# Two transformer blocks on one core: the mixing norm's scale applied where its products are read, the SSD far product half a piece later, gated rows turned by halves

## What is computed

```
hn = rmsnorm(h, norm_mix_w)                    # h * rsqrt(mean(h^2) + 1e-5) * w
q, k, v, z, xbc, dt_raw = split(hn @ w_in)     # 512, 512, 512, 1024, 1536, 16 columns
att = chunk_band_attention(q, k, v, rel_bias)
xbc = silu(causal_depthwise_conv(xbc, conv_w, conv_b))       # x, B, C
dt  = softplus(dt_raw + dt_bias);  a_cum = cumsum(dt * -exp(a_log))
y   = ssd_scan(x, dt, A, B, C) + d_skip * x    # products in chunks with decay
y   = y * silu(z)
y   = y by 2 groups of 512 * rsqrt(mean(y^2) + 1e-5) * norm_w     # the gated rows
h   = h + concat(att, y) @ w_out
h   = h + relu(rmsnorm(h, norm_mlp_w) @ w_ff1)^2 @ w_ff2
out = rmsnorm(h, norm_final_w)
```

## Time and profile before

| | |
|---|---|
| median of 3 runs | 780.57 us |
| runs | 780.35 to 781.04 us |
| the profiled execution | 780.67 us, span 778.9 us |
| granted PE clock | 0.998 of full |
| busy: PE, DVE, ACT, POOL | 762.0, 513.8, 416.0, 98.3 us |
| mixing norm to the turn of the gated rows | 434 to 548 us of the span |

### The profile page before, as it was taken

One profiled execution on the slowest core, in us unless ns is written; L12 is line 12 of the kernel. 1 busy time (PEld: TensorE's weight loads), 2 busy tenths in 40 slices (PEclk: granted clock), 3 DMA queues, 4 the chain that ended last, 5 costly groups with the idle time before them and its releaser, 6 DMA issues.

```text
span 778.9 us, 12960 instructions
## 1 busy us (share of the span) xinstructions
PE 762.0 (98%) x5014; PEld 670.3 (86%) x5014; DVE 513.8 (66%) x816; ACT 416.0 (53%) x623; POOL 98.3 (13%) x74
## 2 busy tenths in 40 slices
PE   8999999999999999999999899999999999999997
PEld 7998877799978887999787699889777999999996
DVE  6985556666664558477866875787856755555554
ACT  5544445453664553446675567576655544444443
POOL 3341000000100004111300207700000000000002
PEclk9999999999999999999999999999999999999999
DMA  9965643344664544676833554765317575656541
GB/s 334 332 203 177 215 163 108 122 157 121 210 224 160 172 157 160 195 227 197 247 114 104 166 176 151 219 205 173 109 55 219 192 237 191 207 177 211 169 156 55
DMA packets 77659, 139.54 MB, mean 179 GB/s; under 512 B 7184, under 2 KB 15648, under 8 KB 77600
## 3 DMA queue, kind: packets, MB, share of 16 engines
q1 hardware_dynamic: 75744, 132.15, 52.4%
q0 software_dynamic: 1856, 6.57, 2.6%
HBM read 134.90 MB, written 1.06 MB: 175 GB/s over the span
## 4 chain that ended last, share of the span: by engine, by line
PE 87%; DVE 6%; issue 3%; POOL 2%; ACT 1%; DMA 1%; SPq 0%; POOLq 0%; ACTq 0%; DVEq 0%
PE acc L1081 13%; PE acc L1083 13%; PE acc L1082 13%; PE acc L1089 12%; PE acc L1091 12%; PE acc L1090 12%; DVE w_lo L810 2%; PE acc L1369 1%; PE acc L1403 1%; DMA raw<-in_w_in_even 1%; PE acc L1342 1%; PE acc L1282 1%; PE acc L1238 1%; PE acc L1353 1%; POOL b_lo L810 1%
## 5 line engine op out<-in xcount | busy, mean ns | idle before, releaser
L810 DVE TENSOR_TENSOR w_lo<-raw,w_hi 128x1024 fp32r<-128x1024 f32 (+1 forms) x224 | 275.3, 1245 | 171.3 <-ACT w_hi L790 90.2
L1089 PE MATMUL acc<-x_hi,w_hi 128*128 128x256 f32 x840 | 234.8, 280 | 1.5 <-DVE w_lo L810 1.1
L1091 PE MATMUL acc<-x_hi,w_lo 128*128 128x256 f32 x840 | 232.1, 276 | 0.0
L1090 PE MATMUL acc<-x_lo,w_hi 128*128 128x256 f32 x840 | 232.1, 276 | 0.0
L790 ACT ACTIVATE w_hi<-raw 128x1024 fp32r<-128x1024 f32 (+1 forms) x128 | 133.6, 1045 | 126.4 <-PE acc L1091 63.9
L780 ACT ACTIVATE w_hi<-raw 128x1024 fp32r<-128x1024 f32 x109 | 116.1, 1065 | 107.6 <-PE acc L1091 55.5
L1089 PEld LDWEIGHTS acc<-x_hi,w_hi 128*128 128x128 f32 x840 | 157.7, 188 | 4.1 <-issue 2.8
L1090 PEld LDWEIGHTS acc<-x_lo,w_hi 128*128 128x128 f32 x840 | 157.8, 188 | 0.8 <-issue 0.5
L1091 PEld LDWEIGHTS acc<-x_hi,w_lo 128*128 128x128 f32 x840 | 157.7, 188 | 0.0
L1081 PE MATMUL acc<-w_hi,cat_hi 128*128 128x512 f32 x272 | 108.9, 400 | 0.2 <-DVE w_lo L810 0.2
L1083 PE MATMUL acc<-w_hi,cat_lo 128*128 128x512 f32 x272 | 106.2, 390 | 0.0
(11 more groups left out here) (297 smaller groups left out, 903.0 us busy)
## 6 DMA issues: line engine op xcount, KB each, us to landing
raw<-in_w_ff SPq DMA_DIRECT2D x32, 1024.0 KB, 5.3
raw<-in_w_in_even SPq DMA_DIRECT2D x28, 1024.0 KB, 5.0
raw<-in_w_in_odd SPq DMA_DIRECT2D x16, 1024.0 KB, 5.4
raw<-in_w_in SPq DMA_DIRECT2D x16, 1024.0 KB, 5.6
raw<-in_w_out_even SPq DMA_DIRECT2D x12, 1024.0 KB, 5.4
raw<-in_w_out SPq DMA_DIRECT2D x4, 1024.0 KB, 5.3
raw<-in_w_in_even SPq DMA_DIRECT2D x4, 512.0 KB, 6.2
raw<-in_w_ukv_even SPq DMA_DIRECT2D x8, 256.0 KB, 3.2
```

The lines of the kernel that those rows point to most:

```text
L810: ins = eng.tensor_tensor(lo, r, hi.bitcast(F32), ALU.subtract)
L1089: pe.matmul(o, wh[k][:, fs], hi[:, ka, :], start=start and f % 2 == 0, stop=False, skip_group_check=True)
L1090: pe.matmul(o, wh[k][:, fs], lo[:, ka, :], start=False, stop=False, skip_group_check=True)
L1091: ins = pe.matmul(o, wl[k][:, fs], hi[:, ka, :], start=False, stop=stop, skip_group_check=True)
```

## The change

Six things change, all in the second block (and one place of the order, `waiting`, that only concerns it).

1. `mix_turn` turns the unscaled rows of `res`, four tiles to a bank. `row_scaled` is gone. ACT's squares and DVE's mean squares stand behind the splits, POOL takes both roots of the layer norm before both of the mixing norm. The filler is 4 products, ahead of tile 1.
2. r is applied where the products are read. For token-major results (V, z, dt) it is a number for each partition (`mix_r`, for tanh `half_r`). For feature-major ones (convolution, q, k) it is a row, which a product of ones and two diagonals spreads over the partitions (`mix_spread`, one instruction of 256 columns, between the halves of the first convolution chunk; ACT copies it to `r_row`). The convolution's, q's and k's results are now read by DVE.
3. V's products of tile 0's low parts stand between the high ones of tile 1 (`v_rows`); dt is one pass of 256 tokens. The pieces with 256 columns share their place in memory differently (`p.shift`).
4. `ssd_far` is a step of its own behind the second half of the piece around `ssd_rows` 0; on DVE its reading stands behind `masked(0)` and z's product.
5. The gate is two steps: `ssd_gate` (variances and root) and `ssd_scale` (the scalings, in the order 0, 2, 1, 3, behind the piece's second half). `ssd_turn` starts with the first two.
6. The low parts of the two output pieces `w_out`, k0 = 4, are POOL's (`state_out`); DVE's low part of the piece at `ssd_scale` stands behind the scalings, and ACT's high part at `ssd_turn` behind the turned rows' own.

```diff
-BUSY_MIX = (5, 1)
+BUSY_MIX = 4
...
     step("mix_turn", 1)
-    step("rows_of", (rows_pieces["dt"], 0, 0, 8))
     step("rows_of", (rows_pieces["v"], 1, 0, 8))
...
+            step("mix_spread", 0)
             step("dt_sum", c_dt)
...
         two()
+        if ("ssd_rows", 0) in sts:
+            step("ssd_far", 0)
+        if ("ssd_gate", 0) in sts:
+            step("ssd_scale", 0)
...
-            p.shift = (80, 112) if p.chunk.layout == "feat" else (0, 0)
+            p.shift = (80, 112) if p.chunk.layout == "feat" or p.cols == S else (0, 0)
...
+        state_out = [p for p in pieces if p.chunk.acts == "cat2" and p.k0 == 4]
...
-            return 4 if p.chunk.epilogue == "silu_tok" and p.chunk.info["dst"][0] == "zb" else 1 if p.n < 2 else 0
+            return 4 if p.chunk.epilogue == "silu_tok" and p.chunk.info["dst"][0] == "zb" or p in state_out else 1 if p.n < 2 else 0
...
-        waiting = {at for at, (s0, s1) in enumerate(zip(steps, steps[1:])) if s0[0] in ("piece", "rest") and s1[0] in ("scores", "ssd_cb")}
+        waiting = {at for at, (s0, s1) in enumerate(zip(steps, steps[1:])) if s0[0] in ("piece", "rest") and s1[0] in ("scores", "ssd_cb", "ssd_turn")}
...
+                if t == 0:
+                    for b in range(4):
+                        high(0, b)
+                    return
+                for b in range(4):
+                    low(0, b)
+                    high(1, b)
+                for b in range(4):
+                    ins = low(1, b)
...
             def mix_turn(t):
 
                 if t:
-                    pe.wait_ge(*due("mix_lo", 4))
-                    keep_busy(acc[:, v_piece.chunk.pair, 1, :], BUSY_MIX[1])
-                rows = tmp[:, t * D:(t + 1) * D]
+                    keep_busy(acc[:, v_piece.chunk.pair, 1, :], BUSY_MIX)
                 for h in range(2):
-                    pe.wait_ge(*due("mix_scaled", 2 * t + h + 1))
+                    pe.wait_ge(*due("mix_row", 2 * t + h + 1))
...
+                elif kind == "mix_spread":
+                    pe.wait_ge(*due("mix_diag", 1))
+                    own(pe.matmul(aux[:, 3, 0:S], ones, gated[:, 1, :], start=True, stop=True), "mix_spread")
...
                 elif kind == "ssd_turn":
-                    pe.wait_ge(*due("y_gated", 1))
-                    turn_tokens(R2[:, 2048:4096].rearrange("p (t n) -> p t n", t=T), "normed_turned")
+                    for h in range(2):
+                        pe.wait_ge(*due("y_gated", h + 1))
+                        turn_tokens(R2[:, 2048:4096].rearrange("p (t n) -> p t n", t=T), "normed_turned", range(4 * h, 4 * h + 4))
...
             def row_hi(t):
 
                 for b in range(4):
-                    act.wait_ge(*due("mix_turned", 4 * t + b + 1))
+                    act.wait_ge(*due("mix_turned", 2 * t + b // 2 + 1))
...
+                elif kind == "mix_spread":
+                    act.wait_ge(*due("mix_spread", 1))
+                    own(act.activation(r_row, aux[:, 3, 0:S], ACT.Copy), "row_scale")
...
+                    elif c.scaled and c.epilogue == "silu_tok":
+                        act.wait_ge(*due("piece_used", c.pieces[-1].n + 1))
+                        act.wait_ge(*due("mix_half", 1))
+                        for t in range(T):
+                            ins = act.activation(epi_dst(c)[:, t], a2[:, t], ACT.Tanh, scale=half_r[:, t:t + 1])
+                        own(ins, "tanh_ready")
...
                 elif kind == "ssd_turn":
                     turned_hi(TURNS["ssd", 0], ssdn_col, cat2_hi[:, 4:12, :], "normed_hi")
+                    hi_first(act, own, held_hi)
...
-                own(dve.tensor_tensor(y, y, zb[:, i * 512:(i + 1) * 512], ALU.mult))
+                own(dve.scalar_tensor_tensor(y, y, mix_r[:, b:b + 1], zb[:, i * 512:(i + 1) * 512], ALU.mult, ALU.mult))
...
+                            ins = dve.tensor_tensor(conv_in[:, f:f + 2, 3:], a2[:, b, :].rearrange("p (f s) -> p f s", f=2), rows_scale(2), ALU.mult)
...
                     row_add(0, 1)
-                    row_mean_square(0)
                     row_part(0, 1)
                     dve.wait_ge(*due("piece_used", last_out[1].n + 1))
                     row_add(1, 1)
                     row_part(1, 1)
                     row_moments(1)
                     row_centred(1)
-                    row_lo(0, 0, 2)
                     row_normed(1)
-                    row_lo(0, 2, 4)
+                    row_lo(0)
+                    row_mean_square(0)
                     row_mean_square(1)
+                    row_lo(1)
                     low_prep(dt_piece.n)
-                    row_lo(1, 0, 4)
                     low_prep(conv_piece.n)
+                    dve.wait_ge(*due("mix_r", T))
+                    for t in range(T):
+                        ins = dve.tensor_scalar(gated[:, 1, t * P:(t + 1) * P], ident, mix_r[:, t:t + 1], None, ALU.mult)
+                    own(ins, "mix_diag")
+                    own(dve.tensor_scalar(half_r, mix_r, 0.5, None, ALU.mult), "mix_half")
...
                     masked(i)
+                elif kind == "ssd_far":
+                    dve.wait_ge(*due("y_far_ready", 1))
+                    own(dve.tensor_tensor(y_far, aux[:, 2:4, :].rearrange("p c (h n) -> p (c h) n", n=SSD_P),
+                                          ssd_c[:, 7, 16:32].rearrange("p (h n) -> p h n", n=1).to_broadcast([P, 16, SSD_P]), ALU.mult),
+                        "far_read")
+                    own.wait()
+                    own(dve.tensor_tensor(y_ssd[:, 1], y_ssd[:, 1], y_far, ALU.add))
...
+                elif kind == "ssd_scale":
+                    y2 = R2[:, 2048:4096]
                     dve.wait_ge(*due("y_rstd", 1))
-                    for n in range(4):
+                    for n in (0, 2, 1, 3):
                         v = y2[:, n * 512:(n + 1) * 512]
-                        own(dve.tensor_scalar(v, v, ssd_c[:, 3, 12 + n:13 + n], None, ALU.mult), "y_gated" if n == 3 else None)
+                        own(dve.tensor_scalar(v, v, ssd_c[:, 3, 12 + n:13 + n], None, ALU.mult), "y_gated" if n > 1 else None)
+                    low_of(*held_low)
+                    held_low = None
...
                         inverse_root(stats[:, 44 + t:45 + t], stats[:, 36 + t:37 + t], "mix_rstd")
+                    for t in range(T):
                         pool.wait_ge(*due("mix_mean", t + 1))
```

More of the change, by code:

```diff
@@ L141, in __init__ @@
         self.banks = None
+        self.scaled = False
 def plan(w):
@@ L547, in build @@
     by_turn = {c.turn: c for c in chunks if c.turn is not None}
-    READER = {"keep_ranks": "act", "copy_tok": "act", "copy_feat": "act", "conv_in": "act", "copy_dt": "dve"}
+    after_mix = min(c.n for c in chunks if c.epilogue == "copy_dt") - 1
+    for c in chunks:
+        c.scaled = c.acts == "x" and c.n >= after_mix and c.epilogue != "relu2"
+    READER = {"keep_ranks": "act", "copy_tok": "act", "copy_feat": "act", "conv_in": "dve", "copy_dt": "dve"}
     reads = {"act": 0, "dve": 0}
@@ L553, in build @@
             c = s[1]
-            c.reader = "act" if c.info.get("table") == 1 else READER.get(c.epilogue, "dve")
+            c.reader = "act" if c.info.get("table") == 1 else "dve" if c.scaled and c.layout == "feat" else READER.get(c.epilogue, "dve")
             reads[c.reader] += 1
@@ L1483, in _, with row_squares @@
             scratch = probs.rearrange("p a n -> p (a n)")[:, 0:D]
-            def row_squares(t):
-                for h in range(2):
-                    act.wait_ge(*due("mix_row", 2 * t + h + 1))
-                    if t and h == 0:
-                        act.wait_ge(*due("mix_squared", 2))
-                    hs = slice(h * NCOL, (h + 1) * NCOL)
-                    own(act.activation(scratch[:, hs], res[:, t, hs], ACT.Square, scale=D ** -0.5, accum_out=stats[:, 38 + 2 * t + h:39 + 2 * t + h]),
-                        "mix_squared")
+            def row_squares(t, h):
+                act.wait_ge(*due("mix_row", 2 * t + h + 1))
+                if t and h == 0:
+                    act.wait_ge(*due("mix_squared", 2))
+                hs = slice(h * NCOL, (h + 1) * NCOL)
+                own(act.activation(scratch[:, hs], res[:, t, hs], ACT.Square, scale=D ** -0.5, accum_out=stats[:, 38 + 2 * t + h:39 + 2 * t + h]),
+                    "mix_squared")
             def last_squares(t, c0, c1, at):
@@ L1611, in _ @@
                     elif c.epilogue == "conv_in":
-                        act.wait_ge(*due("piece_used", c.pieces[-1].n + 1))
                         act.wait_ge(*due("pad_ready", 1))
-                        for b in range(2):
-                            f = c.info["dst"] + 2 * b
-                            ins = act.activation(conv_in[:, f:f + 2, 3:], a2[:, b, :].rearrange("p (f s) -> p f s", f=2), ACT.Copy)
-                        own(ins, "acc_read_act")
-                        own.wait()
+                        act.wait_ge(*due("acc_read_dve", c.read_count))
```

(4 more changed lines are left out.)

135 lines of the change are left out of this document (82 added, 53 removed).

## The result

The changed kernel takes 784.71 us (median of 6 executions, 783.85 to 786.59) against 780.85 for the kernel before; the ratio is 1.0052, with a 95% interval of 1.0040 to 1.0065. It is slower by 3.9 us. Of this 0.3 us lies outside the span and in no term of the forecast: time less span is 2.1 to 2.2 us in each execution of the changed kernel and about 1.8 in those of the kernel before; why stays open. The forecast was 781.7, with a range of 777.9 to 784.2, and "the same" as the likeliest: the time lies above the range.

A forecast was written before the change was run, and what follows sets the result against it. PE bounds the kernel, busy 762.0 of 778.9 us, so only its waits, filler and own instructions count. -2.9 + 0.46 + 2.1 + 2.1 - 0.6 = +1.15 on 780.57 gives 781.7 us, range 777.9 to 784.2.

The forecast's parts named there:

- Mixing norm: Last output product to first convolution product: turning unscaled rows starts the convolution earlier, -2.9 us (-3.7 to -2.5).
- the dt pass: Mixing norm: one pass of 256 columns takes 1.86 us, bounds 1.0 by instruction count and 2.0 by columns.
- Spread: Spreading the scale: one more product of 256 columns in PE's own line, +0.46 us.
- convolution chain: DVE takes ACT's convolution reads: chain to the decay rows 0.8 us later, PE waits 0.24 more at the turn of `x`.
- First near product: PE waits 2.6 us for DVE's `y_far` behind masked rows, low part and z's product: +2.1 us net.
- The gate: Turn of the gated rows: POOL's low parts hold DVE, PE waits 2.8 us for 0.74 before, +2.1 us.
- The question who wins when both come free together: Gate: whether DVE's scalings or POOL's second low part starts first; without the lock rule, 2.8 us less if DVE's go first.
- Scores: Band scores behind the gate: DVE's two low parts ahead of `cat_lo` go, -0.6 us.
- rival 3: Gate: PE's clock falls from 2.4 to 1.2 GHz, the half piece behind takes twice 2.9 us: 784.6 us, chance 0.13.
- Rivals 1: Gate: POOL holds nobody and the wait goes, 781.7 - 2.8 = 778.9 us, chance 0.17.
- 2: Decay rows come sooner, near wait 0.5 us; with a gate held only once 778.5 us, chance 0.10.

The follow-up runs named there:

- Experiment 8: Changed kernel with the far product's place and the low parts of the two w_out pieces both as before the change: 778.36 us, ratio 0.9962 to the kernel before.
- Experiments 3: Changed kernel with only DVE's reading of the far product moved ahead of the masked rows: 781.18 us, ratio 1.0002 to the kernel before.
- 6: Changed kernel with the far product back at its old place for PE and DVE, ahead of the masked rows: 780.68 us, ratio 0.9991 to the kernel before.
- 10: Kernel before with part 4 of the change alone, the far product a step later: 785.60 us, ratio 1.0057 to the kernel before.
- Experiments 4: Changed kernel with POOL's second low part waiting for DVE's four scalings of the gated rows: 782.62 us, ratio 1.0019 to the kernel before.
- 7: Changed kernel with the low parts of the two w_out pieces on DVE again: 782.12 us, ratio 1.0008 to the kernel before.
- 11: Kernel before with part 6 of the change alone, low parts of the two w_out pieces on POOL: 786.93 us, ratio 1.0076 to the kernel before.
- Experiment 2: Changed kernel with five unread filler products in each of PE's waits, at the first near product and the gate: 782.53 us, ratio 1.0016 to the kernel before.
- experiment 1: Changed kernel unchanged, timed again beside the kernel before: 785.31 us, ratio 1.0054.

## Why the prediction was wrong, point by point

- **Mixing norm, -2.9: right.** -2.74 in the table; the dt pass took 1.86, the value chosen between 1.0 and 2.0. Experiment 8 shows the gain in the whole time.
- **Spread +0.46 and convolution chain: right.** +0.43, and 0.46 at the turn of `x` for a forecast of 0.24; POOL's store of the sums started 0.7 us later against the dt sum, for 0.8.
- **First near product, +2.1: right in place, cause and size.** A wait of 2.64 for 2.6; the two steps add up to 2.19. Experiments 3 and 6 take it away, 10 brings it alone.
- **The gate, +2.1: right in cause, 0.3 too large.** +1.78; 2.57 us of wait for 2.8, by one held scaling of 2.58 and a held product of 1.72. Experiments 4 and 7 take it away, 11 brings it alone. The question who wins when both come free together didn't arise: POOL was ahead by 0.05 us. The rule of the Trainium skill (SBUF — State Buffer, "SBUF: two separate sides"), that the port pair is locked for a whole instruction, agrees: the waiting scaling ended 0.28 us after POOL's 2.35, and in experiment 11 the engines alternated instruction by instruction.
- **Scores, -0.6: right**, -0.7 without the clock.
- **The clock: the step that failed.** The sum had no term for it. It was rival 3, with a chance of 0.13, at the gate alone, and the argument against it was one trace: the longest stretch without products, from 436.71 to 440.24, had passed at full clock. That was one execution's luck: with the same order and the same pause of 1.75 us the clock fell there in the profiles of experiments 10 and 11. (The digit 9 of the profile's page means nine tenths or more, so it couldn't have shown such a fall either.) The sum itself had made two pauses of 2.6 us, longer than any in the part of the trace from which I argued, and I asked only of one what it does to the clock. What came in its place is 1.67 us behind the first near product and 1.39 at the turn in the profiled execution.
- **Where the fall comes.** In all five profiles with the unfilled wait at the first near product the clock fell there, and in four of five with that of the gate. At the near product it fell in the last 0.1 us of the wait, during the products of 64 columns or within 0.6 us behind them, and at the gate within the wait, 0.1 to 1.7 us ahead of the transposes. The rival leaned on the Trainium skill (TensorE: Matmul & The Clock Gate, "Part 4: PE-mode transpose"), by which transposes don't count as busy in the way that products do; by these nine falls transposes aren't needed for one, since none had run since the wait began when the clock fell. The stretch of the mixing norm has them, and no run tells their part in it.
- **The price.** Experiment 2 puts it at 2.8 us on average over the executions; 781.7 + 2.8 is 784.5, for 784.71 measured. That rival 3's own time, 784.6, is as near is luck: it priced one fall at the gate at 2.9 us, and the gate's fall, which began within the wait, cost 1.4.
- **The range.** It ended at 784.2, below rival 3's own 784.6, though the prediction says that it takes in most of that rival. With a term of 0 to 3.1 us for both places it would have held the time.
- Rivals 1 and 2 didn't come: DVE was held, and the decay rows weren't sooner.

## What to carry to other kernels

Where a sum of yours makes the tensor engine stand still for a few microseconds, the stretch behind the wait may run at half speed: add that as a term of its own at every such place, and fill the wait with products that nobody reads if it can't be taken away. One trace in which such a place passed at full clock doesn't clear it: the same place with the same pause fell in two other traces. Look at the mean clocks of all executions and at windows of a few microseconds, not only at the digits of the profile's page. When an engine's reading is moved behind other work, count that work to the waiter; here the reading of a finished product, put ahead of one instruction, was worth 4 us. Work given to GpSimd is not free for VectorE: place it where VectorE reads PSUM or rests, not next to a chain of SBUF instructions for which the tensor engine waits.

## What the runs showed of the hardware beyond the forecast

- The granted clock falls in some executions and not in others with the same code and wait: with the gate's wait of 2.6 us alone, 7 of 11 executions of one kernel (experiment 3) and 3 of 11 of another (6) have a mean of 0.997 or less. It fell behind a pause of 1.75 us too (experiment 10), in a stretch of 3.5 us without products.
- A fall isn't always of one length: behind the first near product the clock was at half from 519.7 to 523.1 in the first profile of the changed kernel and from 515.8 to 522.6 in the second.
- The executions of a kernel with a wait of 2.6 us or more spread over 1.5 to 4.8 us, those of one without over 0.8 to 1.8. The kernel before has no such wait either, and its 26 executions beside experiment 1 spread over 3.3 us, so the spread alone doesn't tell the two apart.
- A VectorE addition with one source in PSUM took 0.69 us beside a running GpSimd low part, and the next instruction, with two large SBUF sources, 1.72 for 0.75.
- The wait at the start (first product at 7.4 to 9.3 us) differs by up to 1.9 us between profiles, as much as most terms of this study.
